# A build-time list scheduler that books its transfers on one shared DMA resource

## What is computed

```python
u = rms_norm(h, g_in) @ w_in                  # (rows, 5376): qA kA vA zA qB kB vB zB gate_A gate_B
qa, ka, qb, kb = (rms_norm per head, gains)   # 8, 2, 8, 8 heads
oa = band_attention(qa, own chunk + 2 chunks before, ALiBi bias, sink)
ob = band_attention(qb, own chunk + 8 chunks before, relative bias)
branch_a = (oa * silu(za)) @ w_o_win
branch_b = (ob * silu(zb)) @ w_o_band
h = h + (sigmoid(ga) * branch_a + sigmoid(gb) * branch_b) @ w_out
gate = sigmoid(rms_norm(h, g_ple) @ w_ple_gate)
return h + gate * (p @ w_ple)                 # and the last keys and values
```

## Time and profile before

| | us |
|---|---|
| median of 3 runs | 1264.57 (1262.55 to 1265.67) |
| the profiled execution | 1260.53 |
| span of its slowest core (core 1) | 1258.7 |
| spans of the eight cores | 1253.0 to 1258.7 |
| PE busy | 1177.9 |
| DVE, ACT, POOL busy | 734.2, 642.8, 462.4 |

### The profile page before, as it was taken

One profiled execution on the slowest core, in us unless ns is written; L12 is line 12 of the kernel. 1 busy time (PEld: TensorE's weight loads), 2 busy tenths in 40 slices (PEclk: granted clock), 3 DMA queues, 4 the chain that ended last, 5 costly groups with the idle time before them and its releaser, 6 DMA issues.

```text
span 1258.7 us, 22204 instructions; the slowest of 8 cores (1253.0 to 1258.7 us)
## 1 busy us (share of the span) xinstructions
PE 1177.9 (94%) x8275; PEld 565.9 (45%) x8275; DVE 734.2 (58%) x1671; ACT 642.8 (51%) x997; POOL 462.4 (37%) x516
## 2 busy tenths in 40 slices
PE   4799999999999998999999999999999999999996
PEld 2455454444444444444444444444444444444443
DVE  3675665555565564656556466565655556666654
ACT  2676455554455453545455454555544555545542
POOL 3743132333333432333333333434423334434440
PEclk9899999999999999999999999999999999999999
DMA  9999222333333233322333333333333423334452
GB/s 188 199 180 171 57 54 68 65 75 74 76 65 82 60 79 66 83 67 63 64 71 83 71 80 72 72 73 67 80 72 71 83 67 82 83 90 97 80 82 86
DMA packets 170250, 106.82 MB, mean 85 GB/s; under 512 B 149024, under 2 KB 154272, under 8 KB 167680
## 3 DMA queue, kind: packets, MB, share of 16 engines
q1 hardware_dynamic: 152608, 71.30, 23.0%
q0 software_dynamic: 17536, 34.12, 17.2%
HBM read 80.56 MB, written 21.50 MB: 81 GB/s over the span
## 4 chain that ended last, share of the span: by engine, by line
PE 73%; DMA 15%; DVE 4%; POOL 3%; issue 3%; ACT 1%; SPq 1%; DVEq 0%; POOLq 0%; ACTq 0%
PE psmm L201 65%; DMA actT<-mbuf 10%; PE pss L201 5%; PE pso L201 4%; DMA actT<-zs 3%; DMA xb<-xe 1%; POOL st L191 1%; POOL zs L191 1%; DMA identb<-ident 1%; DMA kbT<-qkn 1%; DVE zs L191 1%; DVE psmm L191 0%; SPq L191 0%; DVE ET L191 0%; DVE st L191 0%
## 5 line engine op out<-in xcount | busy, mean ns | idle before, releaser
L201 PE MATMUL psmm<-W_in,xT 128*128 128x512 bf16 (+1 forms) x2848 | 650.8, 370 | 3.0 <-DVE qkn L191 2.8
L201 PEld LDWEIGHTS psmm<-W_in,xT 128*128 128x128 bf16 x2848 | 254.1, 98 | 261.4 <-issue 10.2
L191 ACT ACTIVATE ET<-pss 128x1024 bf16<-128x1024 f32 (+1 forms) x220 | 221.4, 1006 | 202.4 <-PE pss L201 200.9
L191 POOL TENSOR_TENSOR st<-st,mhalf 128x8 f32<-128x8 f32 (+1 forms) x174 | 218.3, 1265 | 144.1 <-DVE st L191 141.9
L191 ACT ACTIVATE tg<-psmm,st 128x512 bf16<-128x512 f32 x132 | 90.1, 687 | 191.0 <-PE psmm L201 191.0
L191 POOL TENSOR_TENSOR zs<-ont,zs 128x256 bf16<-128x256 f32 (+1 forms) x132 | 89.0, 675 | 249.7 <-DVE ont L191 241.7
L201 PE MATMUL psmm<-W_out,actT 128*128 128x512 bf16 x528 | 127.6, 390 | 29.0 <-DMA actT<-mbuf 27.8
L191 DVE SCALAR_TENSOR_TENSOR xb<-psmm,xb 128x512 f32<-128x512 f32 x132 | 90.6, 687 | 65.5 <-PE psmm L201 65.2
L191 DVE SCALAR_TENSOR_TENSOR psmm<-tg,psmm 128x512 f32<-128x512 bf16 x66 | 45.5, 691 | 136.0 <-PE psmm L201 136.0
L201 PE MATMUL psmm<-W_pg,actT 128*128 128x512 bf16 x528 | 120.7, 379 | 3.0 <-ACT actT L191 1.1
L191 DVE TENSOR_TENSOR qkn<-psmm,st 128x512 bf16<-128x512 f32 (+1 forms) x137 | 80.2, 585 | 45.3 <-POOL st L191 41.6
(11 more groups left out here) (104 smaller groups left out, 1248.9 us busy)
## 6 DMA issues: line engine op xcount, KB each, us to landing
y<-xb SPq DMA_DIRECT2D x32, 512.0 KB, 2.8
xb<-xm SPq DMA_DIRECT2D x29, 512.0 KB, 4.0
W_in<-w_in POOLq DMA_DIRECT2D x10, 1024.0 KB, 26.8
xT<-xmT POOLq DMA_DIRECT2D x28, 256.0 KB, 4.6
xb<-xe POOLq DMA_DIRECT2D x2, 1536.0 KB, 13.1
pT<-pmT POOLq DMA_DIRECT2D x32, 64.0 KB, 2.6
W_out<-w_out POOLq DMA_DIRECT2D x2, 1024.0 KB, 62.0
W_pg<-w_pg POOLq DMA_DIRECT2D x2, 1024.0 KB, 58.3
```

The source lines that it names most:

```text
L191: inst = getattr(e, method)(*[_res(a_) for a_ in args], **{k_: _res(a_) for k_, a_ in kw.items()})
L201: last = getattr(e, m)(*[_res(a_) for a_ in a], **{k_: _res(a_) for k_, a_ in k.items()})
```

## The change

The model of transfers is another one; nothing else. A transfer now has a size in time, `xfer`: 0.4 us for a transpose, otherwise at least 0.3 us and its bytes (four an element) at 250 kB/us. The simulation keeps a time `dma_free` at which the one DMA resource is free. A transfer starts there or 0.6 us after its issue, whichever is later, holds the resource for `xfer`, and lands 0.9 us after that; a transpose lands `MARGIN` = 1.5 us later still. Transfers with a fixed arrival set `dma_free` to 1 us before that arrival. The latencies given at the calls (`lat_override`) are ignored; `lat` becomes 1.5 us plus `xfer` and counts only in the path lengths of the last tiles and for transfers with a fixed arrival.

```diff
@@ top
-LAT_T = 1.9
+MARGIN = 1.5
@@ Sched.ins
             cost = (1.2 if method == "dma_start_transpose" else 0.45) if eng == "sp" else 0.8
             nbytes = n * out.shape[0] * 4
-            lat = 2.5 + nbytes / 150e3
-            if lat_override is not None:
-                lat = lat_override
+            xfer = 0.4 if method == "dma_start_transpose" else max(0.3, nbytes / 250e3)
+            lat = 1.5 + xfer
...
-        return self.op(eng, fn, r=r, w=w, dma=dma, cost=cost, lat=lat, arr=arr)
+        o = self.op(eng, fn, r=r, w=w, dma=dma, cost=cost, lat=lat, arr=arr)
+        if dma is not None and o is not None:
+            o.xfer = xfer
+        return o
@@ Sched.reschedule
+        dma_free = 0.0
...
             t1 = t0 + o.cost
             free[e] = t1
-            tail = (0.16 if e == "pe" else 0.0) + max(t1 + o.lat, o.arr)
+            o.land = max(t1 + o.lat, o.arr)
+            if o.dma is not None:
+                if o.arr:
+                    dma_free = max(dma_free, o.arr - 1.0)
+                else:
+                    dma_free = max(dma_free, t1 + 0.6) + o.xfer
+                    o.land = dma_free + 0.9 + (MARGIN if o.xfer == 0.4 else 0.0)
+            tail = (0.16 if e == "pe" else 0.0) + o.land
@@ dmaT
-              dma=("tr_" + dres[0], 1), lat_override=LAT_T)
+              dma=("tr_" + dres[0], 1), lat_override=1.9)
```

More of the change, by code:

```diff
@@ L92 @@
     __slots__ = ("eng", "fn", "deps", "dma", "signal", "val", "sem", "order", "cost", "lat", "users", "ndeps",
-                 "ready", "start", "path", "tag", "prio", "arr", "pre", "bufs")
+                 "ready", "start", "path", "xfer", "land", "tag", "prio", "arr", "pre", "bufs")
 class Sched:
@@ L118, in op @@
         o = _Op()
-        o.cost, o.lat, o.arr, o.pre = cost, lat, arr, None
+        o.cost, o.lat, o.arr, o.pre, o.xfer = cost, lat, arr, None, 0.0
         if arr and eng == "pool":
```

## The result

The changed kernel takes 1210.1 us (median of four runs, 1209.2 to 1211.5) against 1264.6 us for the kernel before (the median given above), a ratio of 0.9573 (95% interval 0.9553 to 0.9592). The profiled execution fell from 1260.5 to 1209.5 us, by 51.0 where the sum had 20. Executions in which the cores of a die ran at a lower granted clock are left out of every time and ratio here, three of five for the run with a margin of 2.0 us, which so has no ratio.

What follows compares the result with a forecast made beforehand. PE was taken to bound the kernel, with only its idle time behind transposes to win: 1260.5 - 27 + 7 = 1240.5 us, plus 4.0 for the median, told as 1245 us, range 1228 to 1272.

Steps and rivals of the forecast that it cites:

- What bounds the kernel: PE, busy 1177.9 of 1258.7 us; only its idle time can shrink, 33.9 of 36.7 us in 280-1100 behind transposes.
- Part (1): A lone transpose's modelled landing goes from 3.1 to 4.6 us; of 33.9 us of PE waits 27 go, 7 remain.
- (2): Booking all transfers on one DMA resource: up to 2.1 us more distance for some transposes, by itself costing nothing.
- part (4): Loads believed to land sooner move ACT's square of xb earlier: nothing, or -1 to +3 us.
- Part (3): Whether PE has other work to fill the distance, 6.6 us a tile, given free PSUM banks: 7 us come back.
- PE's busy time 1178 +-2: Sign that the forecast is right: PE's total busy time stays unchanged after the change.
- Banks: Rival: transpose waits return as waits for PSUM banks, -5 us, 1260; chance 0.20 together with no effect.
- Slower: Rival: next tile's pieces take the banks before W_out and W_pg, +24 us, some 1289, or 1267; chance 0.18.
- Not doing what it says: Rival: other resources than landings set the modelled order, which hardly changes, 1264.6 us; counted within a shared chance of 0.20.
- All waits gone, 1227: Rival: every mbuf and zs transpose wait of PE goes and nothing comes back, -37.9 us; chance 0.07.
- The page's rule: DMA engines take turns between queues, a packet at a time, so booking one transfer behind the other is wrong in kind.

Runs made afterwards that it cites:

- Putting the collision back: Changed kernel in its own order, each xT load made to wait for the addition writing mbuf's first half, so it goes out with the first mbuf transpose: 1215.4 us, 0.9579.
- load latencies alone: Changed kernel with margin 0 and no shared resource, so only the shorter load and store latencies differ from the kernel before: 1277.2 us, 1.0079.
- The old order with late transposes: Kernel before in its own order, two small stores from SP put in front of each mbuf transpose: ratio 1.0568, some 1336 us.
- the margin alone: Kernel before with the modelled DMA transpose latency raised from 1.9 to 3.4 us, load latencies old, nothing shared: 1228.7 us, 0.9704.
- the old order without collisions: Kernel before in its old order, xT and xb loads of later tiles cut to 128 of 1024 columns: 1217.2 us, 0.9598.

## Why the prediction was right in sign and wrong in size

**What bounds the kernel: right.** PE, and only its idle time behind transposes; these waits went, and the even part got its gain.

**Part (1), what the distance covers: mis-sized by 6.9 us.** I left 7 of 33.9 us for landings over 4.6 us. None stayed. The size followed from its premise: in the chain of waits of before, what the landings of this stretch take over 4.6 us adds to 6.0 us. The premise failed. I took the landings of before as given, while the new order also moves the loads: 3.9 us before the transpose, so that the long landings aren't there. Of `mbuf` transposes the median stayed 2.4, but the longest fell from 6.5 to 4.7 us. (Of `zs` transposes the longest rose from 4.5 to 5.8, without a wait.) Putting the collision back gave 2.7 us of waits and not 7, so the distance alone would have covered most of the 7: it can be more than the 4.6 us asked for (5.6 in the tile shown). I wrote that the booking (2) costs or gives nothing by itself. Without a margin it gives 1277 to 1217, by the runs, and part (4), also put at nothing, costs 0.8% when it comes alone. Nor does a transpose beside a load always cost 1 to 3 us of PE, as I wrote: the 35 shown waits of before are 0.21 to 2.99 us long, with a median of 1.0.

**Part (3), the 7 us that come back: 0.** The free bank seen in the earlier trace rows was the right row, and the bound of one wait a tile was never near. The run with a margin of 3.0 us asks for 3 x 3.0 + 2.1 = 11.1 us of other work a tile for the 6.6 of part (3), and finds it.

**The price of a wait, a term the sum didn't have: some 11 us.** The waits of the kernel before between its two `y` stores add to 36.7 us, in 33 pieces; they cost 47.8 us. Two things stand between. First, the idle time shown begins at the modelled end of a matmul, 0.38 us behind its start, though the next could have followed after 0.217. The run with load latencies alone gives the size of it, for its waits are short (1.8 us at most) and its clock is full: its 22 tiles take 809.84 us, 60.2 more than the changed kernel's, for 50.1 us shown in 46 waits, 0.22 us more for each; 33 x 0.22 = 7.3 us. Second, behind some of the long waits PE runs at a lower granted clock. The kernel before, PE at such a place, and the granted clock (third last column) of the 6 us before and behind:

```profile
532.43 1.03 PE L201 MATMUL psmm<-W_in,xT 128*128 128x256 bf16 x6
536.45 4.97 PE L201 MATMUL psmm<-W_out,actT 128*128 128x512 bf16 x16 [2.99 <-DMA actT<-mbuf]
```

```profile
530.00:536.00 6.00, 3.46 (x24) 1.63 (x22) 3.74 (x10) 3.69 (x7) 2.54 (x3) 0.98 0.68 90
536.00:542.00 6.00, 5.55 (x29) 2.42 (x30) 1.17 (x2) 0.10 (x1) 1.07 (x2) 0.73 0.00 0
```

Sixteen W_out matmuls take 4.97 us where the earlier trace rows has 3.63: a clock of 0.73, between the 2.4 GHz level and the 1.2 GHz level over the 6 us. The slowest core has three such groups (4.97, and 5.31 behind waits of 1.94 and 2.10 us), 4.7 us in all. 7.3 + 4.7 = 12.0 us, against 11.1 measured. The old order with late transposes bears both out: against the kernel before, 24 more waits at 0.22 us and 15.7 for 4.7 us in slow groups make 16.3 us, for the 62.8 - 47.0 = 15.8 that its 22 tiles took beyond the shown waits. I had read "0.99, the 2.4 GHz level almost all the time" and not asked where the missing hundredth stood. After the change the even part has 1.00.

So the sum, redone: 33.9 + 2.8 (the waits of the even part for other things, gone too) + 11.1 = 47.8 for the 22 tiles, 3.2 at the ends and around the span, 51.0. Against 20: 6.9 from part (1), 7 from part (3), 2.8 of small waits, 11.1 of price and 3.2 at the ends.

**PE's busy time 1178 +-2: wrong**, it is 1156.1. The lower clock counts as busy, so does the tail of the last matmul in front of each wait, and 156 records are missing. The Trainium skill, Trainium Kernel Development and Optimization, section Performance Expectations, calls matmul busy time a bad metric, since matmuls are pipelined, and points to the share of the weight loads. The trace agrees: for the same 8275 weight loads PE's busy time fell by 21.8 us, PEld's changed by 4.0, and it is the count of weight loads in 820 us, 5462 to 5804, that has the gain.

**The rivals.** Banks: no. Slower: no; but a slower kernel was one term away, the load latencies alone. Not doing what it says: no. All waits gone, 1227: this happened, and was priced at what is shown.

**The page's rule.** Transposes and loads from two queues slow each other whichever was issued first: 4.65 us for the one issued before the load, 5.0 for xT in the run with the collision put back, where the changed kernel has 3.9. It fits the taking of turns that the Trainium skill's DMA: Bandwidth & Descriptors, section Queues, rings and completion order, states. I had concluded from it that a booking in series is wrong in kind and alone gives nothing. The conclusion was wrong. The two runs without a margin show what the booking moves. Without it, W_ob starts at 860.25, eight `W_in` matmuls that still read the old xT follow it, and the xT load goes at 864.41, in the middle of two `mbuf` transposes that are issued from 862.98 to 865.56. With it, they stand in front of W_ob (857.96), and the xT load goes at 857.15, 3.6 us ahead. That the late foreseen `zs` landing behind the xb load is what puts them there is my reading of the planner, not tested.

**What stays open.** The kernel with short latencies and margin but no booking (1211) still has an xb load 0.5 us ahead of a `zs` transpose in seven of its 22 tiles, and no wait: again the distance. Why none of its xT loads goes within 1.4 us of an `mbuf` transpose, and so none makes the meeting of three that the margin alone (1229) has in seven tiles, I can only tell by its rows, not by a rule; it may be chance. The small difference between the old order without collisions (ratio 0.9598) and the changed kernel (0.9573) isn't assigned.

## What to carry to other kernels

A planner's distance in front of a consumer should come from the landing of a transfer in company, not alone: 2.4 us alone, mostly 4 to 5.5 beside one load (once 6.5), 5.4 to 8.1 between two. Before trusting a forecast from waits, ask what moves besides the wait (here the load that caused it moved too), and where PE is the bound, price its waits at about 1.3 times what the profile shows: a fifth of a microsecond more for each, and 1.3 to 2.8 us more for those of 1.7 us and longer behind which the clock is lower. Here that was three of the kernel before's and nine of the run with late transposes, by no rule that I can give.

## What the runs showed of the hardware that was not expected

A DMA transpose of 128 x 512 bf16 elements with a 512 KB load just before it and a 256 KB load just behind took 8.07 us from issue to landing, for 2.4 alone. Behind waits of 1.94, 2.10 and 2.99 us PE's sixteen matmuls took 5.31, 5.31 and 4.97 us for 3.63; behind 2.62 us, in the old order with late transposes, they took 3.63. And 820 us of PE without a gap the profile shows is possible on this chip with all eight cores at work, at a granted clock of 1.00.
